# Expert matrices stored partition by partition in a two-layer backbone on one core

## The reference

```python
def hier_moe(h, w_rg, w_re, w_gate, w_up, w_down):
    ...                                   # top-1 group of 4, top-2 of its 8 experts, weights w
    order = jnp.argsort(flat_e)
    tok = order // TOP_K
    xs = h[tok]
    a = lax.ragged_dot(xs, w_gate, sizes)       # w_gate, w_up: 32 experts, 1024 x 512
    u = lax.ragged_dot(xs, w_up, sizes)
    y = lax.ragged_dot(jax.nn.silu(a) * u, w_down, sizes)   # w_down: 32 experts, 512 x 1024
    y = y * w.reshape(-1)[order][:, None].astype(y.dtype)
    return jax.ops.segment_sum(y, tok, num_segments=n)
```

## Time and profile before

| | |
|---|---|
| median of three runs | 5001.29 us (5000.02 to 5009.46) |
| span of the profiled execution | 5002.1 us |
| TensorE, matmul / weight load | 4544.4 us (91%) / 3776.1 us (75%) |
| VectorE, ScalarE, GpSimd | 3310.6, 2464.5, 1192.3 us |
| DMA | 1088.92 MB in 581798 packets, mean 218 GB/s |
| expert matrices in it | 438 loads of 1 MB |
| mean granted TensorE clock | 0.959 |

### The profile page before, as it was taken

One profiled execution on the slowest core, in us unless ns is written; L12 is line 12 of the kernel. 1 busy time (PEld: TensorE's weight loads), 2 busy tenths in 40 slices (PEclk: granted clock), 3 DMA queues, 4 the chain that ended last, 5 costly groups with the idle time before them and its releaser, 6 DMA issues. The chain is left out here.

```text
span 5002.1 us, 75983 instructions
## 1 busy us (share of the span) xinstructions
PE 4544.4 (91%) x25973; PEld 3776.1 (75%) x25973; DVE 3310.6 (66%) x5272; ACT 2464.5 (49%) x3056; POOL 1192.3 (24%) x921
## 2 busy tenths in 40 slices
PE   6999998889999897999967999999999987999995
PEld 4887877777877875877745878888877866788774
DVE  6653667676776567777777626677756436877776
ACT  3223555564233315777743225655633222777774
POOL 3650004400000013333334620043000001333333
PEclk8999999999999998999988999999999998999998
DMA  5645234264554566999995635253556345999998
GB/s 188 206 120 122 65 87 104 100 185 139 209 201 168 207 210 262 397 397 397 397 357 169 199 113 117 63 124 97 136 191 217 113 167 174 388 397 397 397 397 330
DMA packets 581798, 1088.92 MB, mean 218 GB/s; under 512 B 111876, under 2 KB 265380, under 8 KB 578552
## 3 DMA queue, kind: packets, MB, share of 16 engines
q1 hardware_dynamic: 531952, 919.40, 54.8%
q0 software_dynamic: 36272, 119.42, 6.6%
q10 hardware_dynamic: 13400, 47.85, 2.4%
HBM read 903.12 MB, written 183.43 MB: 217 GB/s over the span
## 5 line engine op out<-in xcount | busy, mean ns | idle before, releaser
L1800 PE MATMUL merge_acc<-ahead_wide,merge_w_split 128*128 128x512 f32 (+1 forms) x2880 | 638.7, 377 | 20.5 <-DMA ahead_wide<-hT 14.9
L1800 PEld LDWEIGHTS merge_acc<-ahead_wide,merge_w_split 128*128 128x128 f32 x2880 | 505.4, 190 | 128.6 <-issue 18.7
L648 PE MATMUL project_proj_acc<-ahead_wide,project_hT 128*128 128x512 f32 x2280 | 562.1, 399 | 3.0 <-DVE ahead_wide L471 1.7
L2502 DVE TENSOR_TENSOR experts_w_gate<-experts_raw_gate,experts_w_gate 128x2048 fp32r<-128x2048 f32 x146 | 363.4, 2495 | 295.8 <-ACT experts_w_gate L2398 295.8
L648 PEld LDWEIGHTS project_proj_acc<-ahead_wide,project_hT 128*128 128x128 f32 x2280 | 426.1, 191 | 94.0 <-DVE project_hT L501 4.6
L2377 POOL TENSOR_TENSOR experts_w_down<-experts_raw_down,experts_w_down 128x2048 fp32r<-128x2048 f32 x73 | 355.9, 4876 | 512.5 <-ACT experts_w_down L2398 512.5
L2549 PE MATMUL experts_gate_acc<-experts_w_gate,experts_rowsT 128*128 128x512 f32 x1752 | 432.2, 403 | 13.2 <-DVE experts_rowsT L2507 6.9
L964 DVE TENSOR_REDUCE attend_stat<-attend_scores 128x1 f32<-128x1280 f32 (+2 forms) x288 | 305.7, 1061 | 205.9 <-PE attend_scores L865 202.2
L2563 PE MATMUL experts_result_acc<-experts_w_down,experts_hiddenT 128*128 128x512 f32 x1752 | 430.1, 401 | 12.2 <-DVE experts_w_down L2502 12.2
L2549 PE MATMUL experts_up_acc<-experts_w_up,experts_rowsT 128*128 128x512 f32 x1752 | 420.6, 395 | 0.0
L2549 PEld LDWEIGHTS experts_gate_acc<-experts_w_gate,experts_rowsT 128*128 128x128 f32 x1752 | 327.0, 190 | 101.5 <-issue 22.0
(11 more groups left out here) (257 smaller groups left out, 8298.5 us busy)
## 6 DMA issues: line engine op xcount, KB each, us to landing
experts_raw_gate<-in_w_exp_gate_dram SPq DMA_DIRECT2D x146, 1024.0 KB, 13.8
experts_raw_up<-in_w_exp_up_dram SPq DMA_DIRECT2D x146, 1024.0 KB, 12.8
experts_raw_down<-in_w_exp_down_dram SPq DMA_DIRECT2D x146, 1024.0 KB, 11.4
ahead_rows<-in_w_merge_dram SPq DMA_DIRECT2D x120, 768.0 KB, 6.4
merge_mod_w_ada<-in_w_ada_rows_dram POOLq DMA_DIRECT2D x80, 512.0 KB, 3.7
qk<-project_staged SPq DMA_DIRECT2D x74, 512.0 KB, 3.4
ye<-ahead_rows ACTq DMA_DIRECT2D x73, 512.0 KB, 6.3
attend_keys<-qk SPq DMA_DIRECT2D x96, 320.0 KB, 5.6
```

What stands on the lines that cost most here:

```text
L648: m = pe.matmul(acc[g % 2][:, :], hT[:, a, q * KP + k, t * P:(t + 1) * P], w_split[n % SLOTS][:, c, k, :], start=(q == 0 and i == 0 and k ...
L1800: m = pe.matmul(acc[:, b, 0:w], w_split[b][:, a, k, :], hT[:, x, k, 0:w], start=(i == 0 and k == 0), stop=(i == 2 and k == KD - 1))
L2502: dve.tensor_tensor(w[n][:, 1, half, :], raw[n][:, half, :], w[n][:, 0, half, :].bitcast(F32), ALU.subtract).then_inc(w_lo[n].sem, 1)
```

## The change

The host stores the expert matrices in another order, and `expert_half` reads them with the matching pattern. Within each half the rows that one partition takes now follow each other: partition p's 2048 floats are one run of 8 KB. Each half is the same 1 MB at the same place, and what arrives in `raw` is the same, value for value, so that no other line is touched. The order of instructions on every engine is as before.

```diff
@@ expert_half @@
-    return w[l, e, half * rows:(half + 1) * rows, :].rearrange("o (k p) n -> p (o k) n", p=P)
+    return w[l, e, half * rows:(half + 1) * rows, :].rearrange("o (p k) n -> p (o k n)", p=P)
@@ laid_out @@
+    def by_partition(name):
+        w = np.asarray(inputs[name])
+        rows, n = w.shape[2:]
+        halves = w.reshape(DEPTH, NE, 2, rows // (2 * P), P, n).transpose(0, 1, 2, 4, 3, 5)
+        return np.ascontiguousarray(halves).reshape(DEPTH, NE, rows, n)
+
+    return {"w_exp_gate": by_partition("w_exp_gate"), "w_exp_up": by_partition("w_exp_up"),
+            "w_exp_down": by_partition("w_exp_down"),
```

More of the change, by code:

```diff
@@ L2679, in laid_out @@
     two = 2 * KD
-    return {"w_ada_rows0": np.concatenate([w_ada[0][two:], w_ada[1][:two]]), "w_ada_rows1": w_ada[1][two:],
+    def by_partition(name):
[5 more added lines that the diff above has]
+            "w_exp_down": by_partition("w_exp_down"),
+            "w_ada_rows0": np.concatenate([w_ada[0][two:], w_ada[1][:two]]), "w_ada_rows1": w_ada[1][two:],
             "b_ada_columns0": np.concatenate([b_ada[0][two:], b_ada[1][:two]]).T, "b_ada_columns1": b_ada[1][two:].T,
```

## The result

The changed kernel is slower: 5044.9 us, median of four runs (5040.56 to 5048.19), against 5001.99 us for the kernel before, measured beside it (four runs, 5000.02 to 5009.46). The ratio is 1.0085, 95% interval 1.0073 to 1.0097. The profiled execution has a span of 5046.7 us, 44.6 us longer than that of before; the granted clock is the same, 0.959 on the mean. The forecast was 4980 us, with a range of 4975 to 5002. It missed on the wrong side, by rival A in its heavy form.

The account below looks back on a forecast made before the run. The DMA engines were taken to bound the job loops at 18.49 us per job, TensorE next at 18.11. Gains of 9.9 us (layer 0) and 11.3 (layer 1), 21.2 in all, took 5001.3 to 4980 us, range 4975 to 5002.

Parts of the forecast that it names:

- rival A: GpSimd's queue in the job loops: gathered rows come late beside 8 KB packets, 4.8 to 5.4 us delay against 4.8 free.
- heavy form: Gathered rows so late that every job in the loops is longer: above 5011 us, chance 0.12.
- The price of a packet: DMA engines in the job loops: 3.8 ns per packet beside its bytes, 112 fewer per engine and job, saving 0.43 us.
- The sum, 21.2 us: Gain in the two job loops at TensorE's pace: 9.9 us in layer 0 plus 11.3 in layer 1.
- Index 0.6 to 1.2 more: GpSimd's queue: the index load ahead of each gather takes 0.6 to 1.2 us longer beside the long packets.
- Sharing 1.8: The gather's 8 packets per engine, each beside one of 8 KB instead of 2 KB, land 1.8 us later.
- VectorE's step in the way 2.4: A late index puts the gather's issue behind VectorE's turn to the up matrix; landing in 9.5 us, 2.4 more.
- worst case: Gathered rows delayed 5.4 us with 4.4 free at the quick pace: 19.1 us per job, some 5046 us.
- the ring: Closed loop on GpSimd's queue, index load, gather, next index load, which the prediction passed over; 14.1 us before the change.
- B: Job loops: run length doesn't matter in this mixture of reads and writes; pace stays 18.49, 5001 us; chance 0.13.
- C: VectorE's gate step falls on GpSimd's down-matrix step, taking back 5 us: 4985; chance 0.12 shared with a mild rival A.
- D: More than 21 us gained, only if TensorE's own pace depends on the packets; no chance given.

Follow-up runs that it names:

- the lightened kernel of before: Kernel before, index loaded ahead, two of three expert-matrix passes omitted, VectorE and GpSimd low parts for 128 of 2048 columns only: 18.53 and 18.49 us per job.
- down alone: Against the kernel before, only the down matrices in runs of 8 KB, gate and up still in 2 KB runs: 4993.7 us, ratio 0.9977.

## Why the prediction was wrong, point by point

**What bounds the kernel: right.** Two near limits, 18.11 for TensorE and 18.49 for the DMA engines. Two kernels whose gather has slack run at 18.11 from the third job on, and the lightened kernel of before at 18.49 to 18.53.

**The price of a packet: mis-sized.** I took 3.8 ns, from a stretch of 2 us whose 0.82 MB is given to two digits, and called the 10.0 ns of the loop itself an upper end. Measured: 9.2 to 9.4 ns, and 10.6 from down alone. The row from the loop in question was the better one, though its mixture was impure; the row chosen for its purity was short. The Trainium skill's price, some 3 cycles per packet (page "DMA: Bandwidth & Descriptors", section "Why small descriptors are slow (HBM only)"), falls short in this loop as much as my row did, and the measurement decides. Since TensorE caps the gain, the mistake did not touch the sum. It touched the engines: they had 0.65 us of slack per job in hand instead of 0.05, and they were still not what decided.

**The sum, 21.2 us: right as a term.** The kernel with 8 KB runs and the index ahead is at 4983.3, against 5004.5 for the kernel before on the same chip: 21.2 us (14 to 31 by the interval of the ratio). Its two loops are 9.9 and 11.1 us shorter, where the prediction had 9.9 and 11.3. With 4 KB runs it is 17.5 us.

**Rival A: its sum was right, in part by luck, and its chance was wrong.** Index 0.6 to 1.2 more: 0.9 measured. Sharing 1.8: 2.0. VectorE's step in the way 2.4: the step holds the gather's instruction for 0.95 us (1.94 against 0.99), and about 1.0 us more goes with the store, which the prediction didn't name. These are differences of variants, and up to 0.5 us of them is unexplained (with the index ahead the gather lands 0.5 us later with the old runs too). The sum 4.8 to 5.4: 0.88 + 4.12 = 5.0, against 4.82 us free. Its worst case, pace 19.1 and 5046 us, is the number that came, but two mistakes cancel in it. It took 5.4 us of delay, where 5.0 came; and it took 4.4 us as free at TensorE's pace, where the ring leaves 18.11 - 14.1 = 4.0 ("Slack and loop", below).

**The step that failed.** It is the sentence "Against it: the three delays are all taken at their full size, as if none ran beside another". The index load and the gather can't run beside one another. The gather waits for its index, and the next index waits for the gather, so their delays add up by the program's own waits, to 5.0 us. The second reason, that the engines pause when the matrices are ahead, and that this shortens everything in GpSimd's queue, also fell. They pause little: in the changed kernel the DMA share is still 0.98 to 0.99, since the matrices of the next job are asked for as soon as a half is free, and neither index load nor gather got shorter. With both reasons gone, three terms out of rows whose sum exceeds the slack are a forecast, not a rival at 0.12.

**Slack and loop.** The 4.8 us were slack of a phase: 5.0 us of delay would have been 0.2 too many, a pace of 18.7, if the next index load could have started in its old place. It could not, since it waits for the landing. Of the 5.66 us between the two only 4.4 were slack, and all the delays came out of these 4.4. This was readable before in the two timeline rows of GpSimd and the line of `gather` that waits for `x_in`; 5.8 + 7.0 + 1.3 = 14.1 us of a loop of 18.49, plus 5.0 = 19.1.

**B, C and D.** B and C were wrong as written. The runs matter more than forecast, not less. VectorE's gate steps do fall on GpSimd's step (a mean of 3378 ns for one, 2495 before), and cost nothing: with the index ahead VectorE is busier still and the pace is TensorE's. D didn't come: nothing ran below 18.1 with all its work.

## What to carry to other kernels

Where several queues share the DMA engines packet by packet, a longer run for one is a longer turn for all others: before lengthening a bulk transfer's runs, list the small transfers beside it and find those that wait for each other in a ring, add that ring up, and compare the sum, not each member, with the pace. If it is near, break the ring (load the next index ahead) or take the run length at which the bulk limit is already out of the way; here 4 KB was enough. And of two rows for a price take the one from the loop in question.

## What the runs showed of the hardware

- A packet costs 9.2 to 9.4 ns beside its bytes in this loop: 397 GB/s with 2 and 4 KB, 410 with 4 KB, 420 with 8 KB runs. That is more than twice the 3.8 ns of the short stretch of 2 KB runs.
- A transfer of 512 bytes took 5.0 us to land beside 2 and 4 KB runs, 4.6 beside 4 KB and 6.0 beside 8 KB runs (medians); a gather of 128 rows 7.0, 7.8 and 11.3. With 8 KB runs and the index ahead, out of VectorE's way and ahead of the store, the gather took 9.3.
- A gather issued while VectorE subtracts for a low part holds GpSimd until 0.85 to 0.89 us after that subtraction's end (281 gathers); with none running the instruction takes 0.97 to 1.03 us (584 gathers).
- The issue of a transfer on ScalarE's queue does not wait for the casts ahead of it in the program: it went out at 2192.47, and the casts ran from 2192.67 to 2196.4. What has to come later needs a wait.
- One store of 512 KB, issued with the gather or 7 us behind it, goes with 53 us of 5000 when a loop is this near its limit; 1.0 us of each gather and 0.6 of each index load went with it.
